# Seven block products in place of eight for eight of the fourteen input-projection panels of a layer

## The reference

```python
proj = jnp.einsum('btd,de->bte', x, P['w_in'][l])
(xa, ga, qb, kb, vb, ob, ib, fb, qc, kc, vc, gc, qd, fd, id_, gd) = jnp.split(proj, cuts, axis=-1)
ya, ... = rglru_group(xa, ga, ...)
yb, ... = mlstm_group(qb, kb, vb, ob, ib, fb, ...)
yc, ... = retention_group(qc, kc, vc, gc, ...)
yd, ... = hgrn2_group(qd, fd, id_, gd, ...)
out = jnp.einsum('bte,ed->btd', jnp.concatenate([ya, yb, yc, yd], -1), P['w_out'][l])
x = layer_norm(ALPHA * x + out)
x = layer_norm(ALPHA * x + ffn(x))      # layer 0: dense SwiGLU, layer 1: top 2 of 8 experts
```

## Time and profile before

| what | value |
|---|---|
| median of 3 timed runs | 1056.05 us (1053.13 to 1056.63) |
| the profiled execution, its own time | 1044.64 us |
| its span, first to last instruction | 1042.8 us |
| TensorE products busy | 1023.0 us, 98% of the span |
| VectorE / ScalarE / GpSimd busy | 434.4 / 181.8 / 94.3 us |
| mean granted TensorE clock | 0.995 of full speed |
| DMA | 240.17 MB, mean 230 GB/s |

### The profile page before, as it was taken

The page is one execution under the profiler, slowest core; times in us unless marked ns, Lnnn a source line. Parts: engine busy times, 40 slices in busy tenths (PEclk is TensorE's granted clock), DMA queues, the critical chain, the costliest instruction groups (busy, mean ns, idle before and its releaser), DMA issues.

```text
span 1042.8 us, 22726 instructions
## 1 busy us (share of the span) xinstructions
PE 1023.0 (98%) x10341; PEld 740.8 (71%) x10341; DVE 434.4 (42%) x853; ACT 181.8 (17%) x393; POOL 94.3 (9%) x102
## 2 busy tenths in 40 slices
PE   9999999999999999999999999999999999999995
PEld 6787776899999999987877768744545545455552
DVE  5654725555656664148447352621101012010225
ACT  1322223041111100043232231500000000000011
POOL 2000123700000000000011210041000020000010
PEclk9999999999999999999999999999999999999998
DMA  9452238504454235104521429699999999999963
GB/s 334 151 202 82 69 118 301 220 1 162 162 192 162 82 126 228 67 19 143 203 79 44 145 88 367 252 325 357 422 407 409 416 402 408 425 421 424 424 262 113
DMA packets 36548, 240.17 MB, mean 230 GB/s; under 512 B 4768, under 2 KB 8096, under 8 KB 16736
## 3 DMA queue, kind: packets, MB, share of 16 engines
q1 hardware_dynamic: 26896, 216.40, 53.0%
q0 software_dynamic: 6416, 19.52, 5.4%
q10 hardware_dynamic: 3136, 2.75, 0.8%
HBM read 228.60 MB, written 13.07 MB: 232 GB/s over the span
## 4 chain that ended last, share of the span: by engine, by line
PE 93%; DVE 4%; ACT 1%; DMA 1%; issue 1%; SPq 0%; DVEq 0%
PE ps L669 72%; PE ps L1169 14%; PE ps L1274 5%; PE ps L672 1%; DMA up_slots<-in_w_in 1%; DVE x L1992 1%; DVE overlay L1987 0%; ACT overlay L1598 0%; DVE overlay L2123 0%; DVE up_slots L2094 0%; DVE mix_or_moe L2121 0%; DVE overlay L2122 0%; ACT L1598 0%; ACT up_slots L1598 0%; DVE tables L2660 0%
## 5 line engine op out<-in xcount | busy, mean ns | idle before, releaser
L669 PE MATMUL ps<-up_slots,mix_or_moe 128*32 128x352 f32 (+2 forms) x3248 | 245.3, 451 | 0.0
L669 PE MATMUL ps<-x,up_slots 128*128 128x288 f32 (+2 forms) x944 | 233.2, 399 | 0.8 <-DMA up_slots<-in_w_in 0.8
L669 PEld LDWEIGHTS ps<-x,up_slots 128*128 128x128 f32 x944 | 168.9, 190 | 50.8 <-issue 8.3
L669 PEld LDWEIGHTS ps<-up_slots,mix_or_moe 128*32 128x32 f32 (+2 forms) x3248 | 106.6, 111 | 130.5 <-issue 128.8
L669 PE MATMUL ps<-overlay,tables 128*32 128x256 f32 (+5 forms) x2020 | 125.6, 375 | 0.3 <-DVE overlay L1981 0.2
L669 PEld LDWEIGHTS ps<-overlay,tables 128*32 128x32 f32 (+2 forms) x2020 | 76.6, 114 | 46.9 <-issue 5.3
L1169 PE MATMUL ps<-overlay,up_slots 128*128 128x144 f32 x704 | 91.2, 286 | 1.2 <-DVE overlay L2479 1.2
L1169 PEld LDWEIGHTS ps<-overlay,up_slots 128*128 128x128 f32 x704 | 88.2, 190 | 1.4 <-issue 1.4
L669 PE MATMUL ps<-overlay,up_slots 128*128 128x128 f32 (+3 forms) x560 | 86.0, 314 | 1.0 <-ACT overlay L1598 1.0
L2699 DVE TENSOR_TENSOR mix_or_moe<-mix_or_moe,ps 128x352 f32<-128x352 f32 x24 | 11.2, 517 | 178.3 <-PE ps L669 178.3
L669 PEld LDWEIGHTS ps<-overlay,up_slots 128*128 128x128 f32 x560 | 78.2, 191 | 8.6 <-ACT overlay L1598 1.9
(11 more groups left out here) (329 smaller groups left out, 901.2 us busy)
## 6 DMA issues: line engine op xcount, KB each, us to landing
up_slots<-in_moe_w SPq DMA_DIRECT2D x64, 1408.0 KB, 21.0
overlay<-in_moe_w SPq DMA_DIRECT2D x21, 1536.0 KB, 22.5
up_slots<-in_ffn_w SPq DMA_DIRECT2D x30, 1024.0 KB, 6.9
up_slots<-in_w_in SPq DMA_DIRECT2D x27, 1024.0 KB, 4.9
up_slots<-in_w_out SPq DMA_DIRECT2D x8, 1024.0 KB, 9.3
overlay<-in_moe_w SPq DMA_DIRECT2D x7, 1024.0 KB, 22.4
mix_or_moe<-in_states POOLq DMA_DIRECT2D x6, 512.0 KB, 10.5
out_sample_states<-mix_or_moe POOLq DMA_DIRECT2D x6, 512.0 KB, 6.0
```

The costliest lines, as they stand in the source:

```text
L669: return pe.matmul(o, lhsT, rhs, start=start, stop=stop)
```

## The change

Panels 5 to 12 of each layer (VB, KC, QC, ID, VC, GA, GD, GC; called seven-panels 0 to 7 below) are computed by seven products of 512 x 128 weight blocks with 144 tokens each, instead of 2 x 8 products with 288 tokens. Panels 0 to 4 and 13 stay as they are.

- **Weights.** The host stores such a panel as its four blocks. In SBUF a seven-panel takes seven blocks of 256 KB in one of two buffers. Two SP transfers (`seven_in`) bring them: one writes block 3 of HBM four times (1 MB, blocks 3 to 6), one brings blocks 0 to 2 (768 KB). Then POOL (`panel_sums`) issues three transfers that add as they write: block 2 onto blocks 4 to 6 (768 KB), block 0 onto blocks 3 to 5 (768 KB), block 1 onto block 5 (256 KB). The second waits for the first to land, the third for the second. The third is not waited for on POOL.
- **Tokens.** DVE makes four sums of token halves once a layer (`token_sums`, four operations of 128 x 576).
- **Products.** `seven(q, start, end)` on the PE does products start to end-1 of seven-panel q: four weight chunks each, in groups of 2, 3 and 2 products that share a bank. Product 0 waits for the two loads; product 3 for the first sum transfer, 4 for the second, 6 for the third.
- **Results.** ACT copies a group out (128 x 288, 432, 288), three copies a panel instead of two; DVE makes the two tiles from them in six operations (`panel_outputs`).
- **Buffers.** The buffers of the seven-panels lie over slots 0 to 4, so seven-panel 1 is loaded after tile 9, seven-panel q after the last product of q-2, and three panels of the output projection (until now loaded early) after the last seven-panel.

```diff
-N_IN = 2 * len(ORDER)
+SEVEN = range(5, 13)
+N_SEVEN = len(SEVEN)
+N_IN = 2 * (len(ORDER) - N_SEVEN)
+SEVEN_AT = (5888, 0)
+SEVEN_GROUPS = ((0, 2), (2, 5), (5, 7))
...
+        TX = cut(UPF, 3584, 4, KH, TH)
+        BLOCKS = [[cut(UPF, at + 512 * j, KH, P) for j in range(7)] for at in SEVEN_AT]
+        SEVEN_OUT = [cut(UPF, at, n, TH) for at, n in ((9472, 2), (9760, 3), (6 * 2048 + 9530, 2))]
...
+                def seven_in(q):
+                    b = q % 2
+                    loaded["seven", l, q] = loaded.get(("n seven", b), 0) + 32
+                    loaded["n seven", b] = loaded["seven", l, q]
+                    panel, at = w_in[l][SEVEN.start + q], SEVEN_AT[b]
+                    sp.dma_start(UPF[:, at + 1536:at + 3584].rearrange("p (n w) -> p n w", n=4),
+                                 panel[:, 1536:2048].unsqueeze(1).to_broadcast([P, 4, 512])).then_inc(S[f"sx_in_{b}"], 16)
+                    sp.dma_start(UPF[:, at:at + 1536], panel[:, 0:1536]).then_inc(S[f"sx_in_{b}"], 16)
+
+                for i in range(SEVEN.start):
                     if i >= 2:
                         sp.wait_ge(S["in_ps"], N_IN * l + 2 * i - 2)
                     if l == 0 and i == 0:
@@ -446,14 +478,26 @@
                         sp.dma_start(TB[:, late_tb:], tab[:, late_tb:]).then_inc(S["early_tables_in"], 16)
                     if l == 0 and i == 1:
                         sp.dma_start(TB[:, P:late_tb], tab[:, P:late_tb]).then_inc(S["tables_in"], 16)
-                    if i == 6:
+                    if i == 3:
                         if l:
                             sp.wait_ge(S["down_ps"], 3)
-                        for u in range(3):
-                            refill(2 + u, ("out", l, u), w_out[l][u])
-                    if i == 12:
+                        seven_in(0)
+                sp.wait_ge(S["in_ps"], N_IN * l + 2 * SEVEN.start)
+                seven_in(1)
+                for q in range(2, N_SEVEN):
+                    sp.wait_ge(*seven_group("sx_pe", l, q - 2, 2))
+                    seven_in(q)
+                    if q == 4:
                         sp.wait_ge(*mark("ml_ps", "states", l))
                         refill(5, ("out", l, 3), w_out[l][3])
+                sp.wait_ge(*seven_group("sx_pe", l, N_SEVEN - 2, 2))
+                refill(3, ("in", l, len(ORDER) - 1), w_in[l][len(ORDER) - 1])
+                sp.wait_ge(*seven_group("sx_pe", l, N_SEVEN - 1, 2))
+                refill(2, ("out", l, 0), w_out[l][0])
+                sp.wait_ge(*seven_out(l, N_SEVEN - 1, 1))
+                refill(4, ("out", l, 2), w_out[l][2])
+                sp.wait_ge(S["in_ps"], N_IN * (l + 1))
+                refill(3, ("out", l, 1), w_out[l][1])
...
+                def panel_sums(q):
+                    panel, at = w_in[l][SEVEN.start + q], SEVEN_AT[q % 2]
+
+                    def add(first, last, block):
+                        n = last + 1 - first
+                        pool.dma_start(UPF[:, at + 512 * first:at + 512 * last + 512].rearrange("p (n w) -> p n w", n=n),
+                                       panel[:, 512 * block:512 * block + 512].unsqueeze(1).to_broadcast([P, n, 512]),
+                                       accum_op=ALU.add).then_inc(S[f"sx_sum_{q % 2}"], 16)
+
+                    pool.wait_ge(S[f"sx_in_{q % 2}"], loaded["seven", l, q])
+                    add(4, 6, 2)
+                    pool.wait_ge(*seven_sum(l, q, 0))
+                    add(3, 5, 0)
+                    pool.wait_ge(*seven_sum(l, q, 1))
+                    add(5, 5, 1)
+
+                panel_sums(0)
+                panel_sums(1)
+                panel_sums(2)
                 pool.wait_ge(*mark("ml_ac", "vt", l))
                 values(VM_ML, 0)
+                panel_sums(3)
+                panel_sums(4)
+                panel_sums(5)
                 pool.wait_ge(*mark("lru_dv", "out", l))
                 pool.wait_ge(*mark("hg_ac", "vt", l))
                 values(VM_HG, 2)
+                panel_sums(6)
                 pool.wait_ge(*mark("ret_ac", "vt", l))
                 values(VM_RET, 1)
+                panel_sums(7)
...
+                def seven(q, start, end):
+                    blocks = BLOCKS[q % 2]
+                    b1, b2 = X[:, 0:KH], X[:, KH:KT]
+                    products = ((blocks[0], b1[:, :, 0:TH]), (blocks[1], b2[:, :, 0:TH]), (blocks[2], TX[:, 3]),
+                                (blocks[6], TX[:, 0]), (blocks[4], TX[:, 1]), (blocks[3], TX[:, 2]), (blocks[5], b2[:, :, TH:T]))
+                    for j in range(start, end):
+                        g = 0 if j < 2 else 1 if j < 5 else 2
+                        at = j - SEVEN_GROUPS[g][0]
+                        bank = (3 * q + g) % 2
+                        if j == 0:
+                            pe.wait_ge(S[f"sx_in_{q % 2}"], loaded["seven", l, q])
+                        if at == 0:
+                            if 3 * q + g >= 2:
+                                pe.wait_ge(S["sx_ac"], 3 * N_SEVEN * l + 3 * q + g - 1)
+                            else:
+                                pe.wait_ge(S["in_ev"], N_IN * l + dense(2 * SEVEN.start - 2 + 3 * q + g) + 1)
+                        if j == 2:
+                            pe.wait_ge(S["sx_t"], 4 * l + 4)
+                        if j == 3:
+                            pe.wait_ge(*seven_sum(l, q, 0))
+                        if j == 4:
+                            pe.wait_ge(*seven_sum(l, q, 1))
+                        if j == 6:
+                            pe.wait_ge(*seven_sum(l, q, 2))
+                        w, x = products[j]
+                        for k in range(KH):
+                            last = mm(PS[:, bank, TH * at:TH * at + TH], w[:, k], x[:, k], k == 0, k == KH - 1)
+                        if j + 1 == SEVEN_GROUPS[g][1]:
+                            last.then_inc(S["sx_pe"], 1)
...
                 scores(C_, QB, KB, 1, "ml_ps", "s23")
-                proj_tile(12)
+                seven(1, 0, 3)
                 need("ml_dv", "w01")
                 values(B_, 0, VB, "ml_ps")
                 need("ml_dv", "w23")
                 keys(C_, proj[:, KB:KB + 2], "ml_ps")
-                proj_tile(13)
+                seven(1, 3, 7)
                 need("hg_dv", "m4")
                 need("ml_ac", "vt")
...
+                def seven(q, g):
+                    act.wait_ge(*seven_group("sx_pe", l, q, g))
+                    if N_SEVEN * l + q:
+                        act.wait_ge(*seven_out(l, q - 1, min(g, 1)))
+                    n = SEVEN_GROUPS[g][1] - SEVEN_GROUPS[g][0]
+                    f(SEVEN_OUT[g], PS[:, (3 * q + g) % 2, 0:n * TH].rearrange("p (n t) -> p n t", n=n), ACT.Copy
+                      ).then_inc(S["sx_ac"], 1)
...
+                def token_sums():
+                    if l:
+                        v.wait_ge(S["x_ready"], 4 * KT)
+                    else:
+                        v.wait_ge(S["x_in_0"], 16)
+                        v.wait_ge(S["x_in_1"], 16)
+                    v.wait_ge(S["in_ps"], N_IN * l + 8)
+                    b11, b12, b21, b22 = (X[:, k:k + KH, c] for k in (0, KH) for c in TOKEN_HALVES)
+                    sig(tt(TX[:, 0], b11, b12, SU), S["sx_t"], 4 * l + 1)
+                    sig(tt(TX[:, 1], b22, TX[:, 0], AD), S["sx_t"], 4 * l + 2)
+                    tt(TX[:, 2], b12, b22, SU).then_inc(S["sx_t"], 1)
+                    tt(TX[:, 3], TX[:, 1], b21, SU).then_inc(S["sx_t"], 1)
+
+                (p1, p2), (p4, p5, p6), (p7, p3) = ([a[:, i] for i in range(a.shape[1])] for a in SEVEN_OUT)
+
+                def first_outputs(q):
+                    tile = ORDER[SEVEN.start + q]
+                    v.wait_ge(*seven_group("sx_ac", l, q, 1))
+                    tt(proj[:, tile, 0:TH], p1, p2, AD)
+                    sig(tt(p6, p6, p1, SU), *seven_out(l, q, 0))
+
+                def last_outputs(q):
+                    tile = ORDER[SEVEN.start + q]
+                    v.wait_ge(*seven_group("sx_ac", l, q, 2))
+                    tt(p3, p3, p5, AD)
+                    link(tt(p7, p7, p6, AD))
+                    tt(proj[:, tile, TH:T], p3, p6, SU)
+                    sig(tt(proj[:, tile + 1].rearrange("p (h t) -> p h t", h=2), p7.unsqueeze(1).to_broadcast([P, 2, TH]),
+                           SEVEN_OUT[1][:, 0:2], SU), *seven_out(l, q, 1))
+
+                def panel_outputs(q):
+                    first_outputs(q)
+                    last_outputs(q)
...
-    arrays["w_in"] = _panels(w, [128 * tile + (8 if tile >= QC else 0) for tile in ORDER])
+    panels = _panels(w, [128 * tile + (8 if tile >= QC else 0) for tile in ORDER])
+    blocks = panels[:, SEVEN.start:SEVEN.stop].reshape(DEPTH, N_SEVEN, P, 2, KH, 2, P)
+    order = [blocks[:, :, :, half, :, out] for out, half in ((0, 0), (0, 1), (1, 1), (1, 0))]
+    panels[:, SEVEN.start:SEVEN.stop] = np.stack(order, 3).reshape(DEPTH, N_SEVEN, P, -1)
+    arrays["w_in"] = panels
```

139 lines of the change are left out of this document (80 added, 59 removed).

## The result

On the same chip the changed kernel takes 1203.08 us (median, 1196.42 to 1206.14) against 1054.59 (1052.06 to 1056.63): a ratio of 1.1404, 95% interval 1.1355 to 1.1452, slower. The forecast of 1044 and the range to 1100 are both wrong.

What follows compares the result with a forecast made beforehand. The PE was taken as the bound: 15.0 us saved, cut by late weight sums to 6.0 a layer, 12.0 in all, so 1044.64 becomes 1032.6 profiled, or 1044 us on the median. Range 1037 to 1100.

Steps and rivals of the forecast that it cites:

- The PE term: Seven-panels: seven products of 144 tokens instead of 2 x 8 save 7.5 us a layer, 15.0 in all, at most 17.2.
- the two prices: PE time per instruction: 260.4 ns with 288 tokens, 129.5 ns with 144, so half the tokens cost half the time.
- The tail: From the last seven-panel product to the output projection: as before, 10.6 us.
- ACT and DVE cost nothing: Group copies, token sums and six DVE operations a panel (0.30 and 0.45 us each) stay hidden behind the PE.
- B: Time of a 256 KB adding transfer from POOL's issue until its semaphore releases POOL: 4.8 us, bounds 3.5 and 6.6.
- A: Time of a 768 KB adding transfer from POOL's issue until its semaphore releases POOL: 5.5 us, bounds 4.5 and 8.5.
- L: Time of a seven-panel's two loads, second issue included: 7.0 us.
- the formula of POOL's clock: POOL's waits: 2A + 0.6 us a panel plus 10.9 a layer for values products; last sum ends at 61 + 7(2A + 0.6) + 10.9 + B - 0.6.
- the right rival: Sums become the bound at POOL's second wait and the PE's products 4 and 6, from A = 6.3: 1065 to 1120 us, chance 0.42.
- The mean DMA share of 0.39: DMA engines busy 0.39 of 57 to 172 us before the change, taken as support for hidden sums.
- The clock, a rival: Waits in each seven-panel lower the PE's clock; adds to the slower case, up to 1160 us, no chance of its own.
- busy DVE holds up POOL's transfers: DVE copies may keep GpSimd from writing transfer descriptors, making the sums' slow end likelier; no size given.

Runs made afterwards that it cites:

- x10: x3 with layer 0's first feed-forward panel pair loaded on SP right after the first output-projection panel: 1053.32 us, ratio 1.0004 to the kernel before.
- x9: The kernel before with tiles 10 to 25 of both layers worked as two passes of 144 tokens instead of one of 288: 1053.35 us, ratio 1.0015.
- x3: The changed kernel with no sum transfers and no PE waits for them, loads and products kept: 1040.38 us, ratio 0.9954 to the kernel before.
- x5: The changed kernel with sum transfers that only write, and long rows for them and the single load: 1081.35 us, ratio 1.025 to the kernel before.
- x1: The changed kernel with the three sum transfers only writing, not adding, rows still 2 KB: 1150.54 us, ratio 1.0989 to the kernel before.
- x2: The changed kernel, still adding, with one load of 14 KB rows and large sums of 6 KB rows: 1132.35 us, ratio 1.0815 to the kernel before.
- x6: The changed kernel with 20 idle PE products ahead of each wait for a sum: 1276.97 us, ratio 1.2104 to the kernel before.
- x8: The kernel before with POOL's feed-forward weight sums started after two output-projection panels instead of one: 1058.74 us, ratio 1.0051.
- x4: The changed kernel with one 1 MB load a panel and weight sums by four POOL additions instead of transfers: 1065.35 us, ratio 1.0168 to the kernel before.

## Why the prediction was wrong

- **The PE term held as work, and only in part as time.** Predicted 7.5 us a layer without waits; x10 has 7.1 us less work in layer 0. x9 confirms the two prices. But with the sums left out the mixing stages were shorter by 3.9 and 3.6 us in x3 and by 6.4 and 0.5 in x10, and what is missing there is mostly clock (5.1 and 6.8 us), which the prediction had only as a follower of long waits. The tail too: 10.6 us predicted, 10.8 after (the last product's end at 247.63 to the output projection's start at 258.46).
- **ACT and DVE cost nothing:** held. The six operations took 0.29 to 0.31 and 0.45 us as assumed, and x3 shows no wait of the PE for DVE beyond 0.2 us in its mixing stages.
- **The step that failed is "For B the nearest row is a plain POOL transfer of 256 KB: 4.8; for A one of 512 KB: 4.9, plus 0.6 us for 0.26 MB more = 5.5", with L = 7.0.** A was 8.1 us in an empty queue and 11.8 to 17.4 beside a load; put back into the formula of POOL's clock, 152.3 us for six panels less the values products (10.9) and the issues (3.6), it averages 11.5, twice the 5.5 taken and above the upper bound of 8.5. L was 14.6 us (issued at 55.05, landed at 69.7), of which x3 shows 11.6 without any sum. B was near: 4.0 at the median, but 13.1 for seven-panel 0's third sum, issued behind a load, which is the first of the PE's waits in that stretch. The form of the formula held: with A = 11.5, L landing at 69.7 and B = 4.9 it puts the last sum at 69.7 + 7 x 23.6 + 10.9 + 4.3 = 250, where the product that waits for it started at 246.45 (A is taken from six of these seven panels, so this tests the form, not the size). I had the right rival, the right place and the right point from which it decides, A = 6.3, and gave it 0.42; but its own upper end, 1120 us, or 1160 with the clock, lies below the 1203 measured. The PE's waits for the loads and sums, 50.8 us, passed the 15 us a layer that the prediction had named as proof of that rival.
- **Why A was too small** is three things that the nearest rows did not have. Rows of 2 KB (with what came along with them, above): 6.8 against 4.8 to 5.3 for the same bytes. Adding: 7.3 against the same. Both: 8.1, less than the two prices added up. And company: I priced each transfer alone, while seven of sixteen sums in layer 0 were issued close to a load or behind it and took 10.5 to 17.1 us. The Trainium skill, *DMA: Bandwidth & Descriptors*, section Anatomy of one DMA, has neither rows nor adding in its fit; an estimate from it for 768 KB is 3.8 us, and the nearest of the four is the plain transfer with long rows, at 4.8 to 5.3. The measurements decide.
- **The mean DMA share of 0.39 misled me.** The prediction used it as cover. Twice the packet time for 1.2 times the bytes filled it to 0.75, at a mean of 159 GB/s against the 412 of the earlier trace rows. GB/s divided by the share, an estimate of what a full share would move, is 351 before and 363 in x5, 262 in x3 and 261 in x1 (plain, short rows), 244 in x2 (adding, long rows) and 212 after. So the loads in their new form alone brought the share to 0.64 (x3).
- **Three small slips.** "Loads and sums add 3.6 MB a panel" is about their total; the change adds 2.6 MB a panel (282.19 against 240.17 MB, over 16 panels). The plain POOL rows lie 1.7 to 2.2 us above the rule, not 1.6. And of the 11.4 us between the profiled execution and the median, some 7.2 are likely the two lengths of the last stage, 415.0 and 422.2 us. The forecast rests on none of them.
- **The clock, a rival, was real but not the cause here.** In the changed kernel the chain has no PE in it from 55.03 to 246.45 us, so the 0.78 cost little beyond the waits. (From 217 to 242 us eight instructions of a block product take 2.29 us instead of 1.14, and the PE still reaches the last product 0.19 us before its sum.) In x5 it did cost: its mixing stage 0 ends 20.0 us after x10's with only 7.8 us of waits for loads and sums. The waits row, and its stretches in the columns of the earlier trace rows:

```profile
PE ps L734 <- DMA up_slots<-in_w_seven: 7.8, 6, 2.8
```

```profile
140.00:160.00 20.00, 16.82 (x218) 14.19 (x215) 5.69 (x13) 4.17 (x6) 5.24 (x4) 0.83 0.52 184
160.00:194.50 34.50, 33.42 (x171) 21.23 (x171) 18.70 (x34) 10.92 (x16) 11.62 (x22) 0.75 0.85 297
```

  At mean clocks of 0.83 and 0.75 the busy time of 16.82 and 33.42 us holds, by estimate, 2.9 + 8.4 = 11.2 us of lost work, which with the 7.8 makes 19.0 of the 20.0. In that kernel the clock cost more than the waits it came with. That the waits brought it about is not shown: x6 did not separate the two, and in x3, x9 and x10 the clock fell where the PE had had no wait of over 0.6 us in the 50 us before.
- **The handover was not seen at all:** 7.1 us. The prediction checked that the output projection's panels arrive in time (they are 0.4 to 0.8 us late) but not what else waits behind them, the feed-forward panels and POOL's weight sums, and whom those meet. x8 shows the price of one such meeting, 5.5 us (7.4 in its trace).

What stays open: whether the row length, the repeated block or the second transfer is what slows the loads (11.6 us without sums, 6.6 as one transfer of long rows); what brings the clock down where the PE hardly waits; whether busy DVE holds up POOL's transfers, as the prediction feared, which no run isolates; and whether sums made once and stored in HBM ahead of layer 1 would pay, which was not tried. About 7 us a layer are to be had from the PE at full clock.

## What to carry to other kernels

A gain of one product in eight is small (0.9 us a panel), so the new waits must come to less than a microsecond a panel: price the operands' preparation as a loop with its own clock, in company, before counting the arithmetic saved. The nearest row for a transfer is one with the same row length and kind, not the same bytes; if the trace has none, the upper bound has to be well over the plain rows. And where transfers are moved later, list all that is queued behind them up to the next stage.

## What the hardware showed that I had not expected

- An adding transfer's issue holds POOL for 1.27 us (3 x 512 in rows of 2 KB), 0.86 in one row, against 0.75 and 0.53 for plain ones.
- The same 768 KB take 4.8 to 8.1 us alone by row length and kind; an adding transfer beside a load went to 17.4.
- A sum issued 2.8 us or more ahead of a load was hardly slowed by it (7.7 to 9.0 us to landing), one issued behind it was (10.5 to 17.1).
- DVE beside POOL: 128x144 from 0.31 to 2.33 us, 128x576 from 0.75 to 2.89, and in x4 a copy of 128x288, with one input, from 0.28 to 1.31.
- The clock fell to its lower level, 1.2 GHz, for some us without a wait of the PE of over 0.2 us in the 50 us before (x9, some 1.7 us lost in layer 0), and for 10 us in x10, where it cost layer 1 nearly all of its gain.
- Chips differ: the kernel before took 1045.32, 1053.19 and 1052.2 us in three sessions on three chips. In traces of the third session the PE's weight loads are busy 221 to 224 us from 700 to 1000 us, in those of the first 145 to 148, and the stretch from layer 1's output projection to the end is 6 to 7 us longer.
